# A decoder layer in float32: where the attention weights of a head are transposed

## The reference, cut to what matters

```python
q, k, v = jnp.split(h @ w_in, 3, axis=-1)          # rms norm of q and k per head
z = jnp.einsum('bhqd,bhkd->bhqk', qb, k)
strict = key_pos[None, :] < q_pos[:, None]
log_1m = jnp.where(strict, jax.nn.log_sigmoid(-z), 0.0)
rest = lax.cumsum(log_1m, axis=3, reverse=True) - log_1m
a = jnp.where(strict, jnp.exp(jax.nn.log_sigmoid(z) + rest), 0.0)
o = jnp.einsum('bhqk,bhkd->bhqd', a, v)            # then o @ w_out, residual
```

## Time and profile before

| | |
|---|---|
| median of three runs | 1209.72 us |
| profiled execution, first to last instruction | 1207.7 us |
| what lies around it (median less span) | 2.0 us |
| TensorE matmul busy | 1202.5 us, 100% |
| VectorE | 851.9 us, 71% |
| ScalarE | 582.1 us, 48% |
| GpSimd | 59.5 us, 5% |
| DMA engines, mean busy share | 61.7% |

### The profile page before, as it was taken

The page is one execution under the profiler, slowest core; times in us unless marked ns, Lnnn a source line. Parts: engine busy times, 40 slices in busy tenths (PEclk is TensorE's granted clock), DMA queues, the critical chain, the costliest instruction groups (busy, mean ns, idle before and its releaser), DMA issues.

```text
span 1207.7 us, 14964 instructions
## 1 busy us (share of the span) xinstructions
PE 1202.5 (100%) x5420; PEld 997.4 (83%) x5420; DVE 851.9 (71%) x1104; ACT 582.1 (48%) x719; POOL 59.5 (5%) x101
## 2 busy tenths in 40 slices
PE   9999999999999999999999999999999999999998
PEld 7888888888888888888888888888888888888887
DVE  5897979889689676676587577677666666655554
ACT  6556475565655544443444444444444444444442
POOL 0302011011000200000000000000000000001000
PEclk9999999999999999999999999999999999999999
DMA  8665565655555766666666676666565656565663
GB/s 271 210 189 164 158 201 161 205 165 168 183 168 175 224 193 177 205 191 186 199 193 187 192 207 185 183 207 193 185 203 185 205 181 205 181 205 192 206 212 105
DMA packets 119850, 229.58 MB, mean 190 GB/s; under 512 B 7235, under 2 KB 8821, under 8 KB 119797
## 3 DMA queue, kind: packets, MB, share of 16 engines
q1 hardware_dynamic: 119764, 228.90, 61.7%
q10 hardware_dynamic: 32, 0.01, 0.0%
HBM read 226.78 MB, written 2.10 MB: 190 GB/s over the span
## 4 chain that ended last, share of the span: by engine, by line
PE 89%; DVE 5%; issue 0%; ACT 0%; DVEq 0%
PE acc L1109 87%; DVE w_lo L722 2%; DVE side L940 2%; PE T L1156 1%; DVE squares L787 1%; PE R L1174 0%; PE T L1184 0%; DVE xT_lo L951 0%; PE Z L1156 0%; PE acc L1319 0%; PE acc L1327 0%; ACT w_hi L458 0%; PE T L1166 0%; PE Z L1166 0%; PE T L1142 0%
## 5 line engine op out<-in xcount | busy, mean ns | idle before, releaser
L458 ACT ACTIVATE w_hi<-raw 128x1024 fp32r<-128x1024 f32 x425 | 448.6, 1059 | 540.2 <-PE acc L1109 535.2
L722 DVE TENSOR_TENSOR w_lo<-raw,w_hi 128x1024 fp32r<-128x1024 f32 x425 | 517.7, 1224 | 262.2 <-ACT w_hi L458 259.1
L1109 PE MATMUL acc<-w_hi,xT_hi 128*128 128x512 f32 x1200 | 469.8, 392 | 0.2 <-DVE w_lo L722 0.2
L1109 PE MATMUL acc<-w_hi,xT_lo 128*128 128x512 f32 x1200 | 467.1, 389 | 0.0
L1109 PE MATMUL acc<-w_lo,xT_hi 128*128 128x512 f32 x1200 | 467.0, 389 | 0.0
L1109 PEld LDWEIGHTS acc<-w_hi,xT_hi 128*128 128x128 f32 x1200 | 225.3, 188 | 48.2 <-issue 1.2
L1109 PEld LDWEIGHTS acc<-w_hi,xT_lo 128*128 128x128 f32 x1200 | 225.2, 188 | 47.1
L1109 PEld LDWEIGHTS acc<-w_lo,xT_hi 128*128 128x128 f32 x1200 | 225.4, 188 | 46.1
L1109 PE MATMUL acc<-w_hi,hT_hi 128*128 128x512 f32 x352 | 136.9, 389 | 0.0
L1109 PE MATMUL acc<-w_lo,hT_hi 128*128 128x512 f32 x352 | 136.9, 389 | 0.0
L1109 PE MATMUL acc<-w_hi,hT_lo 128*128 128x512 f32 x352 | 136.9, 389 | 0.0
(11 more groups left out here) (160 smaller groups left out, 630.8 us busy)
## 6 DMA issues: line engine op xcount, KB each, us to landing
raw<-in_sb_w_in SPq DMA_DIRECT2D x93, 512.0 KB, 4.0
raw<-in_ffn_w_gate SPq DMA_DIRECT2D x88, 512.0 KB, 3.7
raw<-in_ffn_w_up SPq DMA_DIRECT2D x88, 512.0 KB, 4.3
raw<-in_ffn_w_down SPq DMA_DIRECT2D x88, 512.0 KB, 4.3
raw<-in_sb_w_out SPq DMA_DIRECT2D x32, 512.0 KB, 3.8
raw<-in_ple_w_gate SPq DMA_DIRECT2D x32, 512.0 KB, 4.6
x<-in_x SPq DMA_DIRECT2D x8, 256.0 KB, 6.4
raw<-in_ple_w_proj SPq DMA_DIRECT2D x4, 512.0 KB, 6.5
```

Source lines behind the costliest of these rows:

```text
L458: act.activation(w_parts[0][:, slot(u), 0:n, :], raw[:, slot(u), 0:n, :], ACT.Copy).then_inc(hi_ready, 1)
L722: dve.tensor_tensor(w_parts[1][:, slot(u), 0:n, :], raw[:, slot(u), 0:n, :], w_parts[0][:, slot(u), 0:n, :].bitcast(F32), ALU.subtract).th ...
L1109: last = pe.matmul(acc[pair][tb][:, :], parts[a][:, c, tb * P:(tb + 1) * P], w_parts[w][:, slot(u), i, :], start=(start and i == 0 and n = ...
```

## The change

The three transposes on TensorE are gone. VectorE turns a head's weights, 128x384, in 32x32 blocks that stay on their band of 32 partitions, in one instruction (`block_weights`, slot 5). The blocks then have to change bands: block (a, b) goes from band a to band b. SyncE does that with 16 DMAs a head, each 32 partitions of 384 bytes from `w_blocks` to `w_side`, eight behind the load of the unit for slot 9 and eight behind that for slot 10. ScalarE (slot 8) and VectorE (slot 8, behind it) make `wT1`, `wT0_hi` and `wT0_lo` from `w_side`. The weighted sum moves from slot 6 to 7. In the groups the heads start at slots 0, 3, 6, 9 as before, in the projection at 0, 2, 3, 5 in place of 0, 2, 4, 6. SyncE's loops over groups and tiles are unrolled.

```diff
-    A_EVERY, B_EVERY = 3, 2
-    W_TURN, W_AT, V_AT = 3, 6, 3
+    A_HEADS, B_HEADS = (0, 3, 6, 9), (0, 2, 3, 5)
+    W_BLOCKS, W_MOVE, W_SPLIT, W_AT, V_AT = 5, 9, 8, 7, 3
@@ SyncE
+            def move_weights(h, i, part):
+                if part == 0:
+                    sp.wait_ge(weight_blocks, h + 1)
+                    if h >= 2:
+                        sp.wait_ge(weight_lo_ready, h - 1)
+                for a in range(part * QN // 2, (part + 1) * QN // 2):
+                    for b in range(QN):
+                        sp.dma_start(w_side[i % 2][b * Q:(b + 1) * Q, a, :, :],
+                                     w_blocks[i % 2][a * Q:(a + 1) * Q, b, :, :]).then_inc(weight_moved[i % 2], 16)
+            def attend(u, g, heads):
+                for h in range(HG):
+                    for part in range(2):
+                        if u == heads[h] + W_MOVE + part:
+                            move_weights(g * HG + h, h, part)
...
+                        load(A0 + g * AU + part * DU + u, ...)
+                        if g > 0:
+                            attend(part * DU + u - A_FROM, g - 1, A_HEADS)
@@ ScalarE
-                act.wait_ge(weight_turned, h + 1)
-                act.activation(wT1[i % 2][:, :], R[:, 2 * P:3 * P], ACT.Copy)
-                act.activation(wT0[i % 2][0][:, :], R[:, 0:2 * P], ACT.Copy).then_inc(weight_hi_ready, 1)
+                act.wait_ge(weight_moved[i % 2], 16 * QN * QN * (h // 2 + 1))
+                act.activation(wT1[i % 2]..., w_side[i % 2][:, :, 2, :], ACT.Copy)
+                act.activation(wT0[i % 2][0]..., w_side[i % 2][:, :, 0:2, :]..., ACT.Copy).then_inc(weight_hi_ready, 1)
@@ VectorE
+            def block_weights(h, i):
+                dve.wait_ge(weight_kept, h + 1)
+                if h >= 2:
+                    dve.wait_ge(weight_moved[i % 2], 16 * QN * QN * (h // 2))
+                dve.transpose(w_blocks[i % 2][:, :, :, :].rearrange("p b k i -> p k b i"),
+                              weight[i][:, :].rearrange("p (k b j) -> p k b j", b=QN, j=Q)).then_inc(weight_blocks, 1)
...
-                    if u == every * h + W_AT + 3:
+                    if u == heads[h] + W_AT + 3:
                         keep_o(g * HG + h)
-                    if u == every * h + W_TURN + 4:
+                    if u == heads[h] + W_SPLIT:
                         weights_lo(g * HG + h, h)
-                    if u == every * h + 3:
+                    if u == heads[h] + W_BLOCKS:
+                        block_weights(g * HG + h, h)
+                    if u == heads[h] + 3:
                         log_terms(g * HG + h, h)
@@ TensorE
-            def turn_weights(h, i):
-                pe.wait_ge(weight_kept, h + 1)
-                pe.wait_ge(weight_lo_ready, h)
-                for b in range(3):
-                    last = pe.transpose(R[:, b * P:(b + 1) * P], weight[i][:, b * P:(b + 1) * P], ident[:, :])
-                last.then_inc(weight_turned, 1)
```

More of the change, by code:

```diff
@@ L168, in trunk @@
             weight = [at_row(f"weight{i}", [P, 3 * P]) for i in range(HG)]
+            w_blocks = [at_row(f"w_blocks{i}", [P, QN, 3, Q]) for i in range(2)]
+            w_side = [at_row(f"w_side{i}", [P, QN, 3, Q]) for i in range(2)]
             p_sb = at_row("p_sb", [P, TB, KP * P])
@@ L234, in trunk @@
         behind_ready = sem("behind_ready")
-        weight_turned = sem("weight_turned")
+        weight_blocks = sem("weight_blocks")
+        weight_moved = [sem(f"weight_moved{i}") for i in range(2)]
         exponent_ready = sem("exponent_ready")
@@ L276, in load @@
                 sp.dma_start(raw[:, slot(u), 0:n, :], src).then_inc(landed[slot(u)], 16)
+            def move_weights(h, i, part):
[12 more added lines that the diff above has]
+                            move_weights(g * HG + h, h, part)
             def group(g, skip=0):
                 for part in range(skip, 3):
-                    columns = w_in[:, part * D:(part + 1) * D][:, bass.ts(g, NT)]
                     for u in range(DU):
-                        load(A0 + g * AU + part * DU + u, part * DU + u, D_UNITS[u], columns)
+                        load(A0 + g * AU + part * DU + u, part * DU + u, D_UNITS[u],
+                             w_in[:, part * D + g * NT:part * D + (g + 1) * NT])
+                        if g > 0:
+                            attend(part * DU + u - A_FROM, g - 1, A_HEADS)
             def load_x(r):
@@ L319, in _ @@
             group(0, skip=1)
-            with nc.Fori(1, GROUPS, engines=[mybir.EngineType.SP], hint_back_edge=True) as g:
+            for g in range(1, GROUPS):
                 group(g)
@@ L323, in _ @@
                 load(B0 + u, u, blocks, w_o[:, t * NT:(t + 1) * NT])
-            with nc.Fori(0, XN - 2, engines=[mybir.EngineType.SP], hint_back_edge=True) as n:
+                attend(u - B_FROM, GROUPS - 1, B_HEADS)
+            for n in range(XN - 2):
                 for u in range(DU):
-                    load(B2 + n * DU + u, u, D_UNITS[u], w_o[:, 2 * NT:][:, bass.ts(n, NT)])
+                    load(B2 + n * DU + u, u, D_UNITS[u], w_o[:, (2 + n) * NT:(3 + n) * NT])
+                    attend(BH + n * DU + u - B_FROM, GROUPS - 1, B_HEADS)
             with nc.Fori(0, FN, engines=[mybir.EngineType.SP], hint_back_edge=True) as j:
@@ L557, in weights_hi @@
             def weights_hi(h, i):
[L559 to L561 removed]
+                act.wait_ge(weight_moved[i % 2], 16 * QN * QN * (h // 2 + 1))
+                act.activation(wT1[i % 2][:, :].rearrange("p (a i) -> p a i", i=Q), w_side[i % 2][:, :, 2, :], ACT.Copy)
+                act.activation(wT0[i % 2][0][:, :].rearrange("p (k a i) -> p k a i", a=QN, i=Q),
+                               w_side[i % 2][:, :, 0:2, :].rearrange("p a k i -> p k a i"), ACT.Copy).then_inc(weight_hi_ready, 1)
             def keep_o(h):
@@ L565, in keep_o, with attend @@
                 act.activation(oT[0][:, bass.ds(h, 1), :].rearrange("p a s -> p (a s)"), O[:, 0, :], ACT.Copy).then_inc(oT_hi_ready, 1)
-            def attend(u, g, every):
+            def attend(u, g, heads):
                 for h in range(HG):
-                    if u == every * h + W_AT + 3:
+                    if u == heads[h] + W_AT + 3:
                         keep_o(g * HG + h)
-                    if u == every * h + W_TURN + 3:
+                    if u == heads[h] + W_SPLIT:
                         weights_hi(g * HG + h, h)
-                    if u == every * h + 4:
+                    if u == heads[h] + 4:
                         weights_of(g * HG + h, h)
-                    if u == every * h + 3:
+                    if u == heads[h] + 3:
                         softplus_of(g * HG + h, h)
@@ L602, in group @@
                             keep_v(g - 1, U0 - 1)
-                        attend(u - A_FROM, g - 1, A_EVERY)
+                        attend(u - A_FROM, g - 1, A_HEADS)
                     for part in range(2):
@@ L622, in _ @@
                     keep_v(GROUPS - 1, B0 - 1)
-                attend(u - B_FROM, GROUPS - 1, B_EVERY)
+                attend(u - B_FROM, GROUPS - 1, B_HEADS)
             for u in range(2 * DU):
@@ L627, in _ @@
                 if u == 0:
-                    attend(BH - B_FROM, GROUPS - 1, B_EVERY)
+                    attend(BH - B_FROM, GROUPS - 1, B_HEADS)
                 for t in range(LAST):
@@ L1185, in weigh, with attend @@
                           skip_group_check=True).then_inc(o_ready, 1)
-            def attend(u, g, every):
+            def attend(u, g, heads):
                 for h in range(HG):
-                    if u == every * h:
+                    if u == heads[h]:
                         scores(g * HG + h, h, g)
                 for h in range(HG):
-                    if u == every * h + W_AT:
+                    if u == heads[h] + W_AT:
                         weigh(g * HG + h, h, g)
-                    if u == every * h + W_TURN:
-                        turn_weights(g * HG + h, h)
             def turn_input(r):
```

4 lines of the change are left out of this document (2 added, 2 removed).

## The result

The changed kernel takes 1279.46 us, the median of 5 runs (1279.11 to 1279.91). The kernel before took 1209.63 us beside it (1209.33 to 1209.78). The ratio is 1.0578, with a 95% interval of 1.0567 to 1.059: 69.8 us slower. The forecast was 18 us slower, and the time lies outside its range.

What follows compares the result with a forecast made beforehand. The prediction took TensorE, busy for the whole span, as the bound. Three groups at +4.2 us (+12.6) and the projection at +5.6 gave +18.2 us, so 1228 us, with a range of 1206 to 1246.

Steps and rivals of the forecast that it cites:

- What is removed, 5.3 us: TensorE's three transposes a head, 0.33 us on the chain, standing there 16 times: 5.3 us saved.
- Block transpose 0.65 us: VectorE's added 128x384 block transpose, one a head, taken at 0.65 us, ends 0.44 and 0.96.
- I take 0.45 for 32 partitions; ends 0.26 ... and 0.52: SyncE's issue pitch in us for each of the 16 moves a head, taken from other DMAs in the trace.
- the loop: In the groups, a late head delays the next through VectorE's queue: one turn 10.9 us against TensorE's 9.36.
- TensorE's own head is 9.36: TensorE's time per head in the groups, 9.36 us; heads 1 to 3 come late, stalling it 3.5 us a group.
- Group's end, +2.0: After head 3's weighted sum, VectorE has 21.5 us of work, TensorE 19.7: TensorE waits 2.0 us more a group.
- Projection: stalls 0.8, 4.3, 1.9: TensorE's waits for late weights of heads 1, 2 and 3 beside the output projection: 7.0 us, net +5.6.
- Loads at nothing: In the groups, weights' loads behind SyncE's moves come up to some 2 us late but cost nothing.
- a cover of 4 us: Time in hand for the weights' loads in the groups, about 4 us, against some 2 us of lateness.
- B: Rival, chance 0.21: SyncE's issues cost 0.52 us because short ones fill the queues beside loads; 1245 us.
- A: Rival, chance 0.17: SyncE's issues are cheap; 1209 us at a pitch of 0.37, 1205.6 at 0.26.
- C: Rival, chance 0.07: issues are cheap, but block transposes and blocked slots eat VectorE's backlog; 1209 us, no change.

Runs made afterwards that it cites:

- one: The changed kernel with 15 of a head's 16 moves left out, waits, block transposes and new slots kept; 1204.31 us, ratio 0.9957.
- four_old_slots: The changed kernel with four DMAs a head, each spreading 32 partitions over 128, in one slot, and head steps as in the kernel before; 1204.53 us, ratio 0.9959.
- eleven: The changed kernel with 5 of a head's 16 moves left out; 1232.13 us, ratio 1.0186.
- eight: The changed kernel with 8 of a head's 16 moves left out; 1212.13 us, ratio 1.0022.
- idle_moves: The kernel before, its TensorE transposes kept, with 16 moves a head added on SyncE into a tile nobody reads; 1239.33 us, ratio 1.0247.
- rows: The kernel before with seven rows of four DMA issues of various shapes and memory sides added after its last store; 1234.84 us.

## Why the prediction was off

The direction and the mechanism were right, the size was not. Step by step:

- **What is removed, 5.3 us.** Right: `one` is 5.2 us faster, `four_old_slots` 5.0.
- **Block transpose 0.65 us.** 0.571 measured, inside its ends. The two copies from SBUF take 0.61 us together (101.38 to 101.99) where 0.54 was taken, the rest 0.43 where 0.42 was; last issue to landing is about 1.8 us where 2.0 was taken. These errors are small, some 0.2 us a turn in all.
- **The step that failed: "I take 0.45 for 32 partitions; ends 0.26 ... and 0.52".** It is 0.63. All the rows behind that bound had HBM on one side; none was within SBUF, and that is what costs 0.17 us more. The trace of before could not show it, but the range could have allowed for it. In the loop 15 issues at 0.18 more are 2.7 us a turn; with the load at 0.58 for 0.37 behind moves, now and then a slower issue (in the first group the eight moves at 102.97 take 1.0 us more than 4.95, those at 136.32 0.5 more), and the rest a little shorter, that is the 13.9 for 10.9. The loop multiplies the error: head 0 of a group comes 2.4 us later than forecast (its `wT_lo` ends at 102.45, the forecast had 100.1), each of the three turns behind it costs 3 us again, some 9, and SyncE's row in the projection, 64 moves long, 64 x 0.18 = 11.5 us. `eleven` stands in for a cheaper issue by having fewer of them: 1279.5 - 1232.1 = 47.3 of the 51.5 us that were missed.
- **"TensorE's own head is 9.36", used three times.** Off by 1.2 us a group. A head has 9.36 us where both scores and a weighted sum fall into it. From the weighted sum of head 0 to that of head 3 fewer scores fall: in `one`, where neither waits, it is 127.97 - 101.04 = 26.9 us, not 28.1. So head 3 is wanted at 127.97 and is weighed at 144.10: 16.1 us later, where the forecast had 3.5. Of these, 11.9 show as waits (1.50, 4.72, 2.39 and 3.24), most of the rest as work at half the clock. In `eleven`, where the issues cost what the forecast took, the groups lie 0.3 to 1.5 us and the projection 3.0 us above the forecast.
- **Group's end, +2.0.** Right: from the weighted sum of head 3 at 144.10 to the next group's first products at 166.14 it is 22.0 us, where TensorE has 19.7 of work: +2.3. VectorE sets it, as forecast: from 145.9 us on it works without a pause, and the `w_lo` that the products at 166.14 need is this one, which ends at 166.09:

```profile
164.86 1.23 DVE L748 TENSOR_TENSOR w_lo<-raw,w_hi 128x1024 fp32r<-128x1024 f32 x1
```

TensorE shows 0.15 us of waiting there, since it had spent the time at half its clock (144.7 to 148.4). So a group is 16.1 + 2.3 - 1.3 = +17.1, and +16.9 to +17.4 is measured.
- **Projection: stalls 0.8, 4.3, 1.9.** The waits before the weighted sums of heads 0, 1, 2 are 1.5, 6.4 and 6.8 us, the last one for `oT_lo`, the carry-over that `eight` shows and the forecast lacked. (The forecast also took off 1.4 us of transposes here, where its own row gives 1.3.)
- **Loads at nothing.** True in the changed kernel. But the reason given, a cover of 4 us, rests on a row of 8.4 us a head; the row is 11.8, and in `idle_moves`, where no loop holds TensorE back, the loads come late.
- **Rivals.** B, "issues of 0.52", was the right one in kind and still short: the true price lay beyond it. Its reason, full queues, fell with `rows`, where the queues were empty and the issues as dear. A fell with the pitch, C with `one`. Without the moves the change would be faster, by `one`, and with 8 of them no slower in the groups: between `eight` and `eleven` the loop begins to bind.

Left open: why an issue within SBUF is dearer, and what the few slower issues wait for. No run took these apart.

## What to carry to other kernels

Price an added DMA by its issue on the queue's engine, with both memory sides as they will be, and if no row of the trace has those sides, let the range reach well beyond the nearest row. Multiply by the count and ask whether it stands in a loop; then the error returns at every turn. Ask also if fewer and larger DMAs do it: the 16 moves of a head became 4 because the engine that turned the blocks could choose its columns, and a change that cost 70 us became one that gives 5.

## What was not expected of the hardware

- An issue on SyncE took 0.59 to 0.60 us with both sides in SBUF, on 1, 32 or 128 partitions alike, and 0.42 to 0.43 from HBM on 32 or 128. But the same 512 KB load from HBM took 0.37 us when SyncE had been waiting before it (89.01) and 0.58 right behind a move (94.59). So what an issue shows can depend on the one before it; no run took that apart.
- A block transpose of 128x384 takes 0.571 us, and 0.875 when it reads every fourth column.
- The granted clock fell by half within and right after TensorE's long waits: in nine stretches of 3.4 to 10.2 us between 114 and 401 us. Two of them (columns as in the windows above):

```profile
114.20:121.00 6.80, 4.12 (x12) 3.54 (x13) 4.24 (x7) 4.20 (x8) 0.00 (x0) 0.50 0.51 165
131.30:134.70 3.40, 3.40 (x10) 2.63 (x9) 3.30 (x7) 0.59 (x2) 0.00 (x0) 0.50 0.49 178
```

That is the 1.2 GHz level, and products follow one another there in 0.43 us, against 0.23 in the stretches at 2.4. The first stretch holds the wait of 4.72 us that ends at 116.88. In before, in `one` and in `four_old_slots`, where TensorE does not wait like this, the clock of these stretches is 1.00. It explains why TensorE is busy for longer with less work: in the first group 76.93 us where it had 71.94. In the changed kernel it costs next to nothing, by its trace: no instruction of TensorE stands in the turn of the loop from 102.45 to 116.83, VectorE sets the group's end, and in the projection TensorE comes slowly (9.07 us for the 6.05 of `one`) to the weighted sum of head 3 at 403.82, whose `wT_lo` ends only at 403.77. TensorE works slowly through time in which it would have waited. Where nothing later is waited for, the clock does cost: 2.9 us in `eight`. No run removed the slow clock by itself.
